# A hybrid gMLP and band-attention step: the norm scaling of va behind the mix, and other places and times for x

## Chip, core and metric

One NeuronCore of a Trainium2 chip runs the whole program. The metric is the device time of one execution in microseconds. The kernel before takes 1076.97 us, the median of three runs (1076.26 to 1078.3).

## What is computed

One layer on 2048 prompt rows and 8 x 16 rows of running streams, 1024 wide, all in float32. The reference, cut to what matters here:

```python
h = einsum('bsd,de->bse', x, w_in)                       # u, va, za, q, k, v, z: 512 columns each
u_a = gelu(u);  v_a = layernorm(gelu(va), ln_v_g, ln_v_b)
mix = einsum('gts,bnsgc->bntgc', tril(w_s), v_a in chunks of 128 rows) + b_s     # 4 groups of 128 channels
a_out = u_a * mix
b_out = band_attention(q, k, v)                          # own 64-row chunk and 8 before, learned bias
out = einsum('bse,ed->bsd', [a_out * silu(za) ; b_out * silu(z)], w_out)
x = layernorm(ALPHA * x + out, ln_g, ln_b)
```

The normalised v_a rows of the 128 stream rows are an output too (gv_out), as are k and v rows. Stream rows use a 16 x 16 corner of each w_s and the first 16 values of b_s.

## The kernel before

A float32 product is made of three in a rounded format: each operand is split by ScalarE into a high part (a Copy with rounding) and by VectorE into a low part (the difference), and TensorE adds high x high, high x low and low x high. Every input block therefore passes ScalarE, then VectorE, before a product can use it.

**Stages.** The rows are cut in 17 tiles of 128 (16 of the prompt, one of the streams).

- *va*: for each tile t, `project_tile` (lines 1647 to 1674) makes x times w_in's va columns, 24 products of 512 columns in two halves h (four blocks of 128 input channels each). Between the halves TensorE does `mix(t - 2)` (lines 1676 to 1685): four small full-precision products, one a group, with w_s transposed. Its PSUM bank alternates between `o_ps` and `out_ps`.
- *First pass*: the columns u, za, k, q, z as ten pairs m of column groups, each a 7-product scheme of Strassen's kind (`product(m, p)`, lines 1687 to 1716, p = 0 to 6) on x transposed, for 1024 rows. A step is one product. The seven combinations of x blocks are made by GpSimd (`sum_x`), those of weights by GpSimd (`sum_w`); both are split as above. The pairs are ("u",0), ("za",0), ("u",2), ("za",2), then k, q, z.
- *v's tiles 0 to 7* with `project_tile`, then the *second pass* (1152 rows, each product in two parts of 288 columns), then *v's tiles 8 to 12*, and tiles 13 to 16 inside the first cycles of the attention, which runs to the end with the output projection.

**Orders written out by hand.** Each engine has its own list of instructions, and semaphores tie them together. What stands where in the lists is what the change touches:

- ScalarE in va (lines 1115 to 1137), for tile t: `copy_mix(t - 2)` (PSUM to the slot `st`, waits until an older mix in that slot is stored), the gelu of tile t, the high half of xt(t + 2, 0), the x pieces planned for t, the high half of xt(t + 2, 1).
- VectorE in va (lines 1404 to 1435): bn_stats (1412), bn_aggr (1414), subtract the mean and multiply with the gain (1416), the low half of xt(t + 2, 0), x pieces, multiply with rstd and add the offset (1425, the norm is then done, semaphore `vn_ready`), the low half of xt(t + 2, 1).
- GpSimd in va (lines 951 to 961): one `sum_x`, the bias of mix(t - 2) (`add_bias_s`, 939), variance plus epsilon (957), the power -1/2 (959).
- SP's queue (lines 703 to 726): the loads of tile t + 2 (595), x for the first pass at t = 0, 2, 5, 8 (601), eight broadcast writes of the relative-bias table to DRAM, `s_skew`, at t = 7 (718), the store of mix(t - 3) to `s_mix` (609).
- In a pass, at step (m, p): unit n = 4m + p - 3 is summed by VectorE once product p is done (`add_sums`, 1360). u units: ScalarE's gelu, then GpSimd's `gate_u` (949) multiplies with `mixb`, the mix loaded back from `s_mix` (619); two buffers alternate, and the load for unit j + 2 is issued after the gate of unit j. za units: tanh on ScalarE (`hand`), two scalings on VectorE (`finish_unit`, 1374 and 1378). Product 1 of the next pair waits for all four sums of the pair, product 6 for the first two. In each step ScalarE and VectorE do `hand` or `finish_unit` first, then the weight splits planned for the step (`step_builds`, lines 1042 and 1334), then the sum.
- x pieces (28 for a pass, split by `xo_high_part` and `xo_low_part`, lines 1054 and 1346): for the first pass 21 in tiles 5 to 15, three in tile 16, four in steps 0 to 3; for the second all 28 in v's tiles 1 to 7 (lines 191 to 197). One group kc of seven pieces needs four sums of GpSimd; a low part waits for all four.
- Token tiles live in three places (`xt_buffer`, 211): 8 KB of `u`, of the `copies`, and, behind tile 8 of v, of the old parameters. For v, tile 0 (8) is loaded in the last pair of the pass, tile 1 (9) after the pass's last sum (lines 751 to 760), since its place is that of the copies.

## Time and profile before

| | |
|---|---|
| median of three runs | 1076.97 us |
| the profiled execution | 1074.96 us |
| its span, first to last instruction | 1073.2 us |
| TensorE matmul busy | 1010.8 us, 94% |
| VectorE busy | 716.9 us, 67% |
| ScalarE busy | 515.6 us, 48% |
| GpSimd busy | 324.6 us, 30% |
| mean granted TensorE clock | 0.979 |

Shares of the whole span mix stages with different limits. TensorE's idle time is 62.4 us in all, and it is read stage by stage: which wait ended last there, and what stood in front of it on the engine waited for.

### The profile page before, as it was taken

How to read it: one execution, taken by the hardware profiler on the slowest of the kernel's cores; microseconds unless marked ns; L12 is line 12 of the kernel's file. 1: busy time of each engine (PE TensorE's matmuls, PEld its weight loads, DVE VectorE, ACT ScalarE, POOL GpSimd, SP SyncE). 2: the span in 40 equal slices, each digit the busy share in tenths (PEclk: the TensorE clock that was granted, in tenths of full speed). 3: DMA queues.
4: the chain of work that ended last, by engine and by line, in shares of the span. 5: the costliest groups of instructions: out<-in, count | busy, mean ns of one | idle time of the engine just before them, and what ended most of it. 6: DMA issues, size and time to landing. Idle time of an engine off the chain costs nothing.

```text
span 1073.2 us, 19266 instructions
## 1 busy us (share of the span) xinstructions
PE 1010.8 (94%) x7456; PEld 865.3 (81%) x7456; DVE 716.9 (67%) x1230; ACT 515.6 (48%) x1018; POOL 324.6 (30%) x269
## 2 busy tenths in 40 slices
PE   7979889999998789999999989999999999999997
PEld 6867677878886569999999977777888888888885
DVE  5959976476565794646555551596777777786765
ACT  5335443334444453333434342575666666666630
POOL 2635753532330834242322200003322222223201
PEclk9998999999999889999999999999999999999999
DMA  6684333346456723323455466575344433433222
GB/s 237 190 232 157 99 108 105 114 121 175 148 145 210 247 94 98 89 92 94 146 175 152 128 200 229 199 261 206 131 149 139 157 133 131 157 121 109 90 80 79
DMA packets 126363, 158.95 MB, mean 148 GB/s; under 512 B 13608, under 2 KB 76224, under 8 KB 126272
## 3 DMA queue, kind: packets, MB, share of 16 engines
q1 hardware_dynamic: 111296, 130.45, 37.8%
q10 hardware_dynamic: 14976, 27.27, 8.0%
q8 instruction: 59, 0.97, 0.4%
q14 instruction: 32, 0.26, 0.1%
HBM read 112.57 MB, written 48.26 MB: 150 GB/s over the span
## 4 chain that ended last, share of the span: by engine, by line
PE 72%; DVE 13%; DMA 6%; issue 3%; ACT 2%; SPq 2%; POOL 1%; ACTq 0%; DVEq 0%
PE s_ps L1713 19%; PE oo_ps L1894 15%; PE pt_ps L1713 9%; PE s_ps L1667 6%; PE oo_ps L1856 6%; PE s_ps L1785 5%; DVE xo_l L1346 4%; PE oo_ps L1713 4%; DMA xt_f<-x_tiles 3%; PE pt_ps L1827 3%; DVE wf L1334 2%; DVE cs L1360 2%; PE s_ps L1894 2%; DVE xt_l L1340 1%; ACT st L1085 1%
## 5 line engine op out<-in xcount | busy, mean ns | idle before, releaser
L1713 PE MATMUL s_ps<-xo_h,wf 128*128 128x288 f32 (+1 forms) x960 | 233.7, 328 | 4.2 <-DVE wf L1334 4.2
L1667 PE MATMUL s_ps<-wp,xt_h 128*128 128x512 f32 x448 | 148.8, 415 | 32.5 <-DVE xt_l L1340 32.0
L1713 PEld LDWEIGHTS s_ps<-xo_h,wf 128*128 128x128 f32 x960 | 164.2, 188 | 17.6 <-DVE xo_l L1346 4.6
L1713 PE MATMUL s_ps<-xo_l,wf 128*128 128x288 f32 (+1 forms) x480 | 157.0, 327 | 0.0
L1667 PEld LDWEIGHTS s_ps<-wp,xt_h 128*128 128x128 f32 x448 | 87.1, 200 | 55.2 <-issue 30.7
L1713 PE MATMUL pt_ps<-xo_h,wf 128*128 128x288 f32 (+1 forms) x480 | 120.8, 329 | 6.8 <-DVE cs L1360 6.6
L1492 DVE CUSTOM_DVE_ANT_1 prob<-s_ps,bias 128x640 f32<-128x640 f32 (+1 forms) x112 | 85.7, 803 | 59.0 <-PE s_ps L1785 59.0
L1228 ACT ACTIVATE prob<-prob,low 128x640 f32<-128x640 f32 (+3 forms) x128 | 97.4, 762 | 45.5 <-DVE low L1492 45.4
L1894 PE MATMUL oo_ps<-wo_h,yh 128*128 128x512 f32 x248 | 100.5, 405 | 0.0
L1334 DVE TENSOR_TENSOR wf<-s,wf 128x512 fp32r<-128x512 f32 x60 | 51.6, 862 | 69.6 <-ACT wf L1042 69.6
L1894 PE MATMUL oo_ps<-wo_h,yl 128*128 128x512 f32 x248 | 97.0, 391 | 0.0
L1894 PE MATMUL oo_ps<-wo_l,yh 128*128 128x512 f32 x248 | 97.0, 391 | 0.0
L1713 PEld LDWEIGHTS pt_ps<-xo_h,wf 128*128 128x128 f32 x480 | 82.3, 188 | 17.2 <-DVE wf L1334 9.0
L1713 PEld LDWEIGHTS s_ps<-xo_l,wf 128*128 128x128 f32 x480 | 90.5, 188 | 6.3
L923 POOL TENSOR_TENSOR s<-a,a 128x512 f32<-128x512 f32 x20 | 26.5, 1323 | 220.3 <-DMA a<-w_pair 220.3
L1667 PE MATMUL s_ps<-wp,xt_l 128*128 128x512 f32 x224 | 91.2, 407 | 0.0
L1334 DVE TENSOR_TENSOR wf<-a,wf 128x512 fp32r<-128x512 f32 x80 | 76.1, 964 | 19.4 <-ACT wf L1042 19.4
L1340 DVE TENSOR_TENSOR xt_l<-xt_f,xt_h 128x512 fp32r<-128x512 f32 x68 | 56.1, 837 | 47.6 <-ACT xt_h L1047 47.6
L1516 DVE TENSOR_SCALAR prob<-prob,rden 128x640 f32<-128x640 f32 (+4 forms) x128 | 79.5, 621 | 4.6
L1713 PE MATMUL pt_ps<-xo_l,wf 128*128 128x288 f32 (+1 forms) x240 | 78.2, 326 | 0.0
L1071 ACT ACTIVATE copy<-s_ps 128x512 f32<-128x512 f32 (+1 forms) x60 | 37.2, 620 | 83.3 <-PE s_ps L1713 83.3
L1002 POOL TENSOR_TENSOR rstd_o<-mv_o,eps 128x1 f32<-128x1 f32 x17 | 3.2, 190 | 235.9 <-DVE mv_o L1567 206.3
(154 smaller groups left out, 2069.1 us busy)
## 6 DMA issues: line engine op xcount, KB each, us to landing
a<-w_pair ACTq DMA_DIRECT2D x80, 256.0 KB, 2.7
xt_f<-x_tiles SPq DMA_DIRECT2D x68, 256.0 KB, 3.3
r<-x SPq DMA_DIRECT2D x17, 512.0 KB, 3.6
s_k<-st SPq DMA_DIRECT2D x32, 256.0 KB, 2.8
s_q<-st SPq DMA_DIRECT2D x32, 256.0 KB, 2.7
q<-s_q SPq DMA_DIRECT2D x16, 512.0 KB, 3.7
k<-s_k SPq DMA_DIRECT2D x16, 512.0 KB, 5.4
y_out<-r SPq DMA_DIRECT2D x15, 512.0 KB, 2.6
```

The source lines that it names most:

```text
L1071: nc.scalar.activation(wide(copies[p // 2], pas), sum_at(p, pas), ACT.Copy).then_inc(copied, 1)
L1228: nc.scalar.activation(prob[s][:, 0:n], prob[s][:, 0:n], ACT.Exp, bias=low[:, s:s + 1], scale=-1.0, accum_out=den[:, s:s + 1]).then_inc(ex ...
L1334: nc.vector.tensor_tensor(wf[:, p, 1], operand[p][:], wf[:, p, 0].bitcast(f32), ALU.subtract).then_inc(w_ready, 1)
L1340: nc.vector.tensor_tensor(xt_l[b][h][:], xt_f[b][h][:], xt_h[b][h][:].bitcast(f32), ALU.subtract).then_inc(xt_ready, 1)
L1346: nc.vector.tensor_tensor(xo_l[a][p][:, kc, :], xo_f[a][p][:, kc, :], xo_h[a][p][:, kc, :].bitcast(f32), ALU.subtract).then_inc(xo_ready, 1)
L1492: nc.vector.tensor_tensor_reduce(out=out, in0=src, in1=b, scale=1.0, scalar=MASKED, op0=ALU.add, op1=ALU.min, accum_out=low[:, s:s + 1]).t ...
L1516: nc.vector.tensor_scalar(prob[s][:, lo:n], prob[s][:, lo:n], rden[:, s:s + 1], None, ALU.mult).then_inc(normed, 1)
L1667: made = nc.tensor.matmul(out, xx[b][h][:, kc % HK, :], wp[:, kc, side, :], start=(h, i, a) == (0, 0, 0), stop=(h, i, a) == (1, HK - 1, 2))
L1713: made = nc.tensor.matmul(out, wf[:, p, side, kc, :], xx[pas][p][:, kc, c * n:(c + 1) * n], start=kc == 0 and a == 0 and p in (0, 1, 3, 5) ...
L1785: last = nc.tensor.matmul(s_ps[h][:, at_c:at_c + count * P], q[t % 2][rows, a * GRP + p, :], key_slots(rows, c * GRP + p, first, count), s ...
L1856: last = nc.tensor.matmul(o_ps[64 * h:64 * h + 64, p * P:(p + 1) * P], v[(t + 1 - nk + b) % KR][:, p * P + 64 * h:p * P + 64 * h + 64], pt ...
L1894: last = nc.tensor.matmul(out_bank(half), y[n % 2][:, c, :], w[h][:, c, :], start=c == 0 and a == 0, stop=c == KC - 1 and a == 2)
```

## The change

- The norm is no longer applied with gain and offset. After the statistics GpSimd also makes shift = -mean * rstd, and ScalarE applies rstd and shift in one instruction (`normalise_va`, ahead of the high half of xt(t + 2, 1)). The gain, a value per channel, commutes with the mix: `scale_mix` multiplies the loaded `mixb` with it on VectorE and adds `mix_b`, which is b_s plus the row sums of w_s times the offset. The row sums are two products of ones with w_s ahead of mix(0); `mix_b` and `mix_bs` (streams) are made on VectorE at its tile 2. GpSimd's bias addition and eight copies for the stream bias go. gv_out gets gain and offset in two VectorE instructions in the first pass's step 1 and is stored from `cs1`.
- x pieces: 16 in va's tiles 3 to 14 and in v's tiles 2, 3, 5, 6; twelve in steps 0 to 3 of each pass. GpSimd makes two `sum_x` a tile; the x loads are at t = 0, 1, 3, 5.
- In a step, ScalarE and VectorE do the splits first, then `hand` or `finish_unit`, then (VectorE) `scale_mix`, then the sum.
- Token halves have seven places. Half 0 of v's tiles 1 and 9 has the place of `mixb`, is loaded in the last pair of the pass and split in its step 4; half 1 is loaded after the last sum but one. The mixes of units 8 and 9 are loaded in v's tiles instead of in the first pass. The first two loads of v for the attention go behind those of tile 12.

The diff, cut:

```diff
+X_FIRST = [(kc, p) for kc in range(HK) for p in range(4)]
+X_REST = [(kc, p) for p in range(4, OPS) for kc in range(HK)]
+for _j, _piece in enumerate(X_FIRST):
+    X_IN_TILE[0].setdefault(3 + 3 * _j // 4, []).append(_piece)
+    X_IN_TILE[1].setdefault((2, 3, 5, 6)[_j // 4], []).append(_piece)
+X_IN_STEP = {step: X_REST[3 * step:3 * step + 3] for step in range(4)}
...
+def xt_place(kind, t, h):
+    if kind == "v" and h == 0 and t in (1, V_MID + 1):
+        return 6
+    if tile_seq(kind, t) % 2:
+        return 2 + h
+    return 4 + h if kind == "v" and t > V_MID else h
...
 (SP)
-                    if j + 2 < len(U_UNITS):
+                    if j + 2 < len(U_UNITS) and j + 2 not in (8, 9):
...
-                    if h == 0 and t in (0, 2, 5, 8):
-                        load_xo(0, (0, 2, 5, 8).index(t))
+                    if h == 0 and t in (0, 1, 3, 5):
+                        load_xo(0, (0, 1, 3, 5).index(t))
...
                             sp.wait_ge(ya_full, 8 * (pas + 1))
+                            sp.wait_ge(u_mixed, 8 * (pas + 1))
                             t = V_MID * pas
                             for h in range(2):
                                 load_xt("v", t, h)
+                            load_xt("v", t + 1, 0)
+                sp.wait_ge(added, 4 * NP * (pas + 1) - 1)
+                load_xt("v", V_MID * pas + 1, 1)
                 store_unit(4 * NP * (pas + 1) - 1)
-                sp.wait_ge(added, 4 * NP * (pas + 1))
-                t = V_MID * pas + 1
-                for h in range(2):
-                    load_xt("v", t, h)
...
-            sp.wait_ge(u_mixed, len(U_UNITS))
-            load_v(0)
-            load_v(1)
             for t in range(V_MID, V_EARLY):
...
+                if t == V_MID + 2:
+                    sp.wait_ge(xt_freed, tile_number("v", V_MID + 1))
+                    load_v(0)
+                    load_v(1)
 (GpSimd)
             for t in range(TILES):
-                if t >= 1:
-                    sum_x(0, t - 1)
-                if t >= 2:
-                    add_bias_s(t - 2)
+                for j in (2 * t - 2, 2 * t - 1):
+                    if 0 <= j < 16:
+                        sum_x(0, j)
                 pool.wait_ge(mv_v_ready, t + 1)
...
+                pool.wait_ge(rstd_v_ready, t + 1)
+                nc.gpsimd.tensor_scalar(shift_v[:], mv_v[:, 0:1], rstd_v[:], -1.0,
+                                        ALU.mult, ALU.mult).then_inc(shift_v_ready, 1)
 (ScalarE)
+            def normalise_va(t):
+                act.wait_ge(shift_v_ready, t + 1)
+                nc.scalar.activation(st[t % 2][:, 0:512], st[t % 2][:, 0:512], ACT.Identity, bias=shift_v[:],
+                                     scale=rstd_v[:]).then_inc(vn_ready, 1)
...
-                    if h == 0 and t < TILES - 1:
+                    if h == 0:
                         for kc, p in X_IN_TILE[0].get(t, ()):
                             xo_high_part(0, kc, p)
+                        normalise_va(t)
...
+                    for what in step_builds(step):
+                        w_high_part(what)
+                    for kc, o in X_IN_STEP.get(step - first, ()):
+                        xo_high_part(pas, kc, o)
                     if p >= 4:
                         hand(4 * m + p - 4)
 (VectorE)
+            def scale_mix(n):
+                if n not in U_COUNT:
+                    return
+                pas, _, g, tb = unit_of(n)
+                j = U_COUNT[n] - 1
+                dve.wait_ge(mix_b_ready, 2 * GRP)
+                dve.wait_ge(mixb_loaded[j % 2], 16 * (j // 2 + 1))
+                held, add = mixb[j % 2][:, 0:512].rearrange("p (n t) -> p n t", t=P), mix_b[:, g, :]
+                made = nc.vector.scalar_tensor_tensor(out=held, in0=held, scalar=v_cols[:, g:g + 1],
+                                                      in1=bass.AP(add.tensor, add.offset, [add.ap[0], [0, 4], [1, P]]),
+                                                      op0=ALU.mult, op1=ALU.add)
+                if pas:
...
+                made.then_inc(mix_scaled, 1)
...
-                nc.vector.scalar_tensor_tensor(out=va, in0=va, scalar=mv_v[:, 0:1], in1=lnvg[:], op0=ALU.subtract,
-                                               op1=ALU.mult).then_inc(vn_centred, 1)
...
-                nc.vector.scalar_tensor_tensor(out=va, in0=va, scalar=rstd_v[:], in1=lnvb[:], op0=ALU.mult,
-                                               op1=ALU.add).then_inc(vn_ready, 1)
                 if t + 2 < TILES:
                     xt_low_part("va", t + 2, 1)
+                if t == 2:
+                    dve.wait_ge(cols_loaded, 32)
+                    dve.wait_ge(row_sums, 2)
+                    for g in range(GRP):
+                        nc.vector.scalar_tensor_tensor(out=mix_b[:, g, :], in0=row_ps[0][:, g * P:(g + 1) * P],
+                                                       scalar=v_cols[:, GRP + g:GRP + g + 1], in1=bs[:, g, :],
+                                                       op0=ALU.mult, op1=ALU.add).then_inc(mix_b_ready, 1)
...
+                    for what in step_builds(step):
+                        w_low_part(what)
+                    for kc, o in X_IN_STEP.get(step - first, ()):
+                        xo_low_part(pas, kc, o)
                     if p >= 4:
                         finish_unit(4 * m + p - 4)
...
+                    if p >= 3:
+                        scale_mix(4 * m + p - 3)
 (TensorE)
                 if t == 0:
                     pe.wait_ge(const_ready, 6)
+                    for row, held in zip(row_ps, (wt, wts)):
+                        nc.tensor.matmul(row[:], st[3][:, 0:P], held[:].rearrange("p g t -> p (g t)"),
+                                         start=True, stop=True).then_inc(row_sums, 1)
                 pe.wait_ge(vn_ready, t + 1)
+                if t == 1:
+                    pe.wait_ge(mix_b_ready, GRP)
```

## Rows read from the trace of the kernel before

**Rows 1.** Busy time by stage: us, PE, PEld, DVE, ACT, POOL, PEclk, DMA, GB/s

```profile
22.60:73.70 51.10, 51.07 (x256) 43.11 (x256) 43.49 (x52) 18.83 (x34) 27.84 (x29) 1.00 0.62 183
...
90.40:133.80 43.40, 39.27 (x192) 31.63 (x190) 42.98 (x48) 20.91 (x38) 28.63 (x28) 1.00 0.40 123
133.80:142.40 8.60, 4.42 (x14) 3.61 (x15) 8.02 (x13) 3.55 (x8) 2.86 (x5) 0.80 0.20 62
142.40:337.70 195.30, 191.73 (x845) 156.44 (x844) 121.94 (x154) 81.87 (x145) 70.72 (x47) 1.00 0.48 141
337.70:404.10 66.40, 50.80 (x194) 39.39 (x192) 52.10 (x52) 32.88 (x58) 32.90 (x19) 0.87 0.52 171
404.10:633.00 228.90, 225.72 (x1689) 224.37 (x1690) 126.36 (x156) 88.51 (x162) 66.45 (x48) 1.00 0.42 125
633.00:672.40 39.40, 32.65 (x138) 25.40 (x136) 11.00 (x20) 13.10 (x24) 0.52 (x1) 0.91 0.69 240
```

**Rows 2.** TensorE's waits over the span: total us, times, longest

```profile
PE s_ps L1667 <- DVE xt_l L1340: 32.0, 9, 7.8
...
PE pt_ps L1713 <- DVE cs L1360: 6.6, 8, 1.0
...
PE s_ps L1713 <- DVE wf L1334: 4.2, 1, 4.2
```

**Rows 3.** Durations of tile st's instructions (ns min/median/max), and one group (mean ns)

```profile
L1412 DVE BATCH_NORM_STATS2 stats_v<-st x17: 673/680/695, 20.3 to 140.2; 128x6 f32<-128x512 f32 x17
...
L1425 DVE SCALAR_TENSOR_TENSOR st<-st,rstd_v,lnvb x17: 736/1757/1781, 23.1 to 142.4; 128x512 f32<-128x512 f32 x17
...
L959 POOL TENSOR_TENSOR rstd_v<-rstd_v,minus_half 128x1 f32<-128x1 f32 x17 | 14.8, 871 | 1.3
```

**Rows 4.** Timeline of va's tiles 2 to 7: start us, us, engine, [idle before]

```profile
29.30 0.60 ACT L1131 ACTIVATE st<-s_ps 128x512 f32<-128x512 f32 x1 [2.14 <-PE s_ps L1667]
...
31.83 1.05 PE L1683 MATMUL oo_ps<-wt,st 128*128 128x128 f32 x8
...
61.04 0.60 ACT L1131 ACTIVATE st<-pt_ps 128x512 f32<-128x512 f32 x1 [1.92 <-PE pt_ps L1667]
```

**Rows 5.** Timeline behind the writes of the bias table

```profile
67.92 3.94 SPq L601 DMA_DIRECT2D xo_f<-x_t  x4
...
77.94 0.60 ACT L1061 ACTIVATE st<-oo_ps 128x512 f32<-128x512 f32 x1 [13.66 <-DMA s_mix<-st]
```

**Rows 6.** Timeline of the first za pair

```profile
175.20 1.77 DVE L1334 TENSOR_TENSOR wf<-a,wf 128x512 fp32r<-128x512 f32 x1
...
177.72 0.47 PE L1713 MATMUL pt_ps<-xo_h,wf 128*128 128x512 f32 x1 [0.88 <-DVE cs L1360]
```

**Rows 7.** First u pair: timeline, the chain's row of product 1, mixb's landing

```profile
155.28 1.75 POOL L949 TENSOR_TENSOR u<-u,mixb 128x512 f32<-128x512 f32 x1
...
158.24 1.75 POOL L949 TENSOR_TENSOR u<-u,mixb 128x512 f32<-128x512 f32 x1
...
161.71 0.68 DVE L1360 TENSOR_TENSOR u<-pt_ps,copy 128x512 f32<-128x512 f32 x1
...
163.24 2.72 PE pt_ps L1713 x12
...
DMA to landing us min/median/max: 2.6/2.7/3.9
```

**Rows 8.** Timeline of v's tiles 1 to 3

```profile
347.98 0.71 PE L1667 MATMUL s_ps<-wp,xt_h 128*128 128x512 f32 x2 [3.66 <-DVE xt_l L1340]
...
351.59 29.24 POOL L905 TENSOR_TENSOR xo_f<-xo_f,xo_f 128x576 f32<-128x576 f32 x16 [34.34 <-DMA xo_f<-x_t]
...
366.69 1.19 PE L1667 MATMUL s_ps<-wp,xt_h 128*128 128x512 f32 x2 [5.92 <-DVE xt_l L1340]
```

**Rows 9.** Timeline of v's tiles 9 and 11

```profile
640.70 1.19 PE L1667 MATMUL s_ps<-wp,xt_h 128*128 128x512 f32 x2 [3.84 <-DVE xt_l L1340]
...
655.87 0.70 PE L1667 MATMUL s_ps<-wp,xt_h 128*128 128x512 f32 x2 [1.50 <-DVE xt_l L1340]
```

More of the change, by code:

```diff
@@ L1150, in _ @@
                         hand(4 * m - 1)
-                    for what in step_builds(step):
-                        w_high_part(what)
-                    for kc, o in X_IN_STEP[pas].get(step - first, ()):
-                        xo_high_part(pas, kc, o)
                     if step == first + 2:
@@ L1398, in _ @@
                 w_low_part(("piece", 0, j))
-            dve.wait_ge(lnv_loaded, 48)
-            for b in range(SB):
-                nc.vector.tensor_copy(bss[:, :, b * SN:(b + 1) * SN], bs[:, :, 0:SN]).then_inc(bss_ready, 1)
+            def scale_mix(n):
[10 more added lines that the diff above has]
+                if pas:
+                    held = mixb[j % 2][:, KEEP:WIDTH[1]]
+                    made = nc.vector.scalar_tensor_tensor(out=held, in0=held, scalar=v_cols[:, g:g + 1],
+                                                          in1=mix_bs[:, g, tb * HALF_S:(tb + 1) * HALF_S],
+                                                          op0=ALU.mult, op1=ALU.add)
+                made.then_inc(mix_scaled, 1)
             for t in range(TILES):
@@ L1444, in _ @@
                         finish_unit(4 * m - 1)
-                    for what in step_builds(step):
-                        w_low_part(what)
-                    for kc, o in X_IN_STEP[pas].get(step - first, ()):
-                        xo_low_part(pas, kc, o)
+                    if p >= 3:
+                        scale_mix(4 * m + p - 3)
                     if m == NP * (pas + 1) - 1 and p in (2, 3):
                         xt_low_part("v", V_MID * pas, p - 2)
+                    if m == NP * (pas + 1) - 1 and p == 4:
+                        xt_low_part("v", V_MID * pas + 1, 0)
                     add_sums(m, p)
@@ L1727, in _ @@
                         pe.wait_ge(xt_high, XT_COUNT["va", t, h])
[L1728 removed]
+                    made = nc.tensor.matmul(tile_ps[t], xt_h[xt_place("va", t, h)][:, j, :], wp[:, kc, 0, :], start=i == 0, stop=False)
                     if i == HK:
@@ L1736, in _ @@
                 for t in range(2):
-                    made = nc.tensor.matmul(tile_ps[t], xt_l[t][h][:, j, :], wp[:, kc, 0, :], start=False, stop=i == KC - 1)
+                    made = nc.tensor.matmul(tile_ps[t], xt_l[xt_place("va", t, h)][:, j, :], wp[:, kc, 0, :], start=False, stop=i == KC - 1)
                     if i == KC - 1:
```

169 lines of the change are left out of this document (85 added, 84 removed).

## The prediction

> **What bounds the kernel now.** I read the table by stage first, then who TensorE waited for, then the timelines of the stages with gaps. The table shows where TensorE is not full [rows 1]. In 22.6 to 73.7 us it is full beside a VectorE busy 43.49 of 51.1 us. In 90.4 to 133.8 VectorE is busy 42.98 of 43.4 us and TensorE 39.27. In 337.7 to 404.1, the first half of v's tiles, TensorE has 50.80 of 66.4 us and a granted clock of 0.87, and in 633.0 to 672.4, the start of the second half, 32.65 of 39.4 at 0.91. The two passes of products are nearly full (191.73 of 195.3, 225.72 of 228.9). So the bound is TensorE, with VectorE taking over in the token stages. The waits say the same: 32.0 us for the low halves of x, 6.6 us in eight waits of about 0.8 us for a sum in the za pairs, 4.2 us once at the first product [rows 2]. Over 0.2%, 2.2 us, can be told from no change here.
>
> A time that recurs below: an undisturbed va tile takes (61.04 - 29.30) / 5 = 6.35 us, its mixing product included [rows 4]. A product takes about 2.8 us in the first pass and 3.2 in the second (195.3 and 228.9 us over 70) [rows 1].
>
> **va's stage, VectorE relieved.** Each tile loses two scalings on VectorE; the second takes 0.74 us alone and 1.76 typically, when GpSimd works beside it [rows 3]. The kept bn_stats takes 0.68, with its aggregate 0.9. The x pieces in this stage fall from 24 to 16, and GpSimd loses its bias addition. VectorE then has at most 0.9 for the statistics, two low halves and two pieces: 0.9 + 4 x 1.76 = 7.9 us at worst, 0.9 + 4 x 0.7 = 3.7 at best, of 6.35. The sixteen GpSimd sums come two a tile up to tile 8 and end there, so from tile 9 the lower figure holds. Six tiles then take 38.1 instead of 43.4 us: gain 5.3. The wait of 4.2 us at the first product goes [rows 2], and with it the low clock: 8.6 us at 0.80 instead of 1.00 are 1.7 us [rows 1]. In tile 8 the low half no longer follows a scaling: 0.8.
>
> What is added lies on ScalarE, the normalising, one instruction of 0.6 us a tile like the others of its size (0.60) [rows 5]. It stands ahead of the high half of xt(t+2, 1) and waits for a chain: gelu 0.6, statistics 0.9, GpSimd's three small instructions 1.3, of which the power is 0.87 [rows 3], normalising 0.6, high 0.6, low 0.7: 4.7, with signals about 5.5 us after a tile's last product. TensorE asks for that half 6.35 + 3.6 = 10 us after it. The cover is 4.5 us; if GpSimd is held by more than that by a late x load, each microsecond beyond is TensorE's.
>
> The Trainium skill, "ScalarE: Activation LUTs", Rules for kernel authors, would leave a multiply and add to VectorE. The stage rows speak for the opposite here, VectorE being the full engine and ScalarE half idle; by the rule the sum would lack the 5.3 us.
>
> **The new wait in tile 3.** mix(1) writes the bank that holds the row sums and so waits until VectorE has made mix_b, which it does at the end of its tile 2, behind both low halves of tile 4. From the gelu of tile 2 at 29.30 [rows 4] the chain of 5.5 us (the gelu included) and four short operations, which I put at 0.25 each (nothing in the trace shows them; below by 0.2, above by 0.7 each), end at 35.8 less signals counted twice, about 35.3. TensorE stood there at 31.83 [rows 4]: 3.5 us. The two row products are 512 columns each like the mix, 0.9 each: 1.8; the earlier start of tile 2 gives 0.8 back. Cost 4.5 us, between 1 and 7. The wait behind s_skew stays: its eight transfers are still queued at tile 7, and ScalarE stood 13.66 us for the store behind them, until 77.94 [rows 5]; x's fourth load is issued at 67.92, behind that store [rows 5], so its move forward frees nothing ahead of it. Net of va: 5.3 + 4.2 + 1.7 + 0.8 - 4.5 = **7.5 us gained**.
>
> **The passes, order of work within a step.** In a za pair VectorE adds, waits for tanh, scales twice, splits a weight and adds again; the split takes 1.77 where GpSimd is beside, and TensorE then waits 0.88 for the sum [rows 6]. The split moves into the wait for tanh, so 0.7 to 1.77 us leave this chain; all 6.6 us of such waits [rows 2] go.
>
> **The passes, the scaling of the loaded mix.** scale_mix now stands on VectorE ahead of the sum, and waits for the load of mixb. That load waits for GpSimd's gate of two units earlier. Today the gates of units 0 and 1 end at 155.28 + 1.75 = 157.0 and 158.24 + 1.75 = 160.0, a load lands 2.7 (2.6 to 3.9) us later, and the sums need none of it [rows 7]. Now unit 2's sum can start at 157.0 + 2.7 + 0.7 = 160.4, unit 3's at 160.0 + 2.7 + 0.7 = 163.4 instead of 161.71, and product 1 of the next pair, which waits until that is done (0.7 more, 164.1), started at 163.24 [rows 7]: 0.9 us in the second u pair of the first pass, none in that of the second, whose steps are longer. In the first pair of a pass twelve x pieces more are split, three a step on ScalarE (3 x 0.55) and VectorE. ScalarE's block loads for the next pair follow them: about 3.4 us later against TensorE, GpSimd's sums and gate behind that. I put 4.0 us in the first pass, where ScalarE also has the last normalising ahead (3.7 us), 0.5 there for the first copy, and 1.5 in the second. Cost 6.9, between 0 and 23 (below). Passes together: **0.3 us lost**. gv_out's two VectorE instructions stand in step 1 and are hidden by product 1 and 2, which need nothing of VectorE's then; without that cover, 1.4. Its store stays on SP at step 2, and behind it only the last mix stores wait.
>
> **v's first half.** Today tile 1 waits 3.66 us for a load issued only when the pass has ended; GpSimd's 16 sums start at 351.59 and take 29.24 us, 1.83 each; VectorE's pieces of the first group stand ahead of tile 3's halves, for which TensorE waits 5.92 us until 366.69 [rows 8]. After: tile 1 is at hand, the sums start some 3 us earlier, VectorE takes xt of tile 3 first and only then four pieces (to 366.8), so that tile 4 is the one that waits, to about 368.7, then tile 5 to 379.6 (4 + 2 operations at 1.83), and the pass starts at about 398 against 404.1. Units 8 and 9's mixes, loaded on SP behind tile 4's halves, are needed only in the second pass, which hides them; ahead of tile 5's halves they would cost about one landing, 2.7. Gain **6.3 us**, between 0 (the slowed pair GpSimd and VectorE still sets the end) and 11.
>
> **v's second half.** The wait of 3.84 at tile 9 goes and so does its low clock [rows 9], but the next tiles then reach the queue of q, k and the bias table earlier: the two v loads of the attention no longer stand ahead of it on SP, and tile 11's load lands about 3 to 4 us earlier, and starts it at about 652.3 instead of 655.87 [rows 9]. Gain **3.6 us**, between 1 and 7.
>
> **Sum.** 7.5 - 0.3 + 6.3 + 3.6 = 17.1. The profiled execution took 1074.96 us (span 1073.2, 1.8 around it), 2.0 below the median of 1076.97; 1074.96 - 17.1 = 1057.9, **1058 us**.
>
> **Rivals.**
> *Port*: scale_mix reads two tiles in SBUF and so may run at 1.76 instead of 0.7 [rows 3] whenever GpSimd sums or gates beside it, as in rows 7. Two in each of four u pairs exposed: 8 x 1.06 = 8.5 us: 1066.5. For it: the gate itself is the neighbour; against: the wait for the load leaves GpSimd idle. The Trainium skill, "SBUF — State Buffer", Who interferes with whom, has exactly this rule, a VectorE instruction with two SBUF inputs blocks against a GpSimd one that reads SBUF; the trace agrees for the old scaling. Chance 0.13.
> *v gives nothing*: the pieces and sums on VectorE and GpSimd still end when they did, the bias table still governs tile 11: 1058 + 9 = 1067. Against it: twelve pieces leave. Chance 0.10.
> *More than I give*: mix_b comes in time and the load chain hides: 4.5 + 6.9 less: 1046.6. For it: half of the costs are estimates. Chance 0.14.
> *Slower*: VectorE's wait for mixb takes the place of all that is saved. Per u pair gate 1.75, load 3.9, scaling 1.76 and sum 0.7 behind block loads that are late too: unit 3 at 17.6 us after product 3 instead of the 10.9 due: 6.7 us, 28 over four pairs instead of my 6.9: 1079. It decides from about 6.5 us a pair. The landing of 2.7 speaks against it. Chance 0.06.
> *No change*: ScalarE, waiting every tile for GpSimd's three small instructions, gives va's gain back and the load chain v's: 1075. Chance 0.04. The forecast itself (1051 to 1065) has 0.53.
>
> **Numbers.** Range 1046 to 1070: it takes in the forecast, both rivals at 1067 and the larger gain, and leaves out slower, no change and the tails. Faster than 1074.8: 0.53 + 0.13 + 0.10 + 0.14 = 0.90; within 0.2% 0.04; slower 0.06.
>
> **What would show it.** Right: no TensorE wait at the first product; a wait of 3 to 4 us at the second mix; VectorE under 0.7 busy in tiles 10 to 16; no eight waits for cs; short waits at product 1 after u pairs; v's pass starts some 60 us after the last product instead of 66. Wrong: TensorE waiting for xt_l in the va tiles behind normalised ones, gaps over 5 us after u pairs, or a v stage as long as now.

## The result, and the profile after

| | before | after |
|---|---|---|
| median | 1077.59 us (1076.26 to 1078.3) | 1069.16 us (1067.01 to 1069.9) |
| ratio | | 0.992, 95% interval 0.9904 to 0.9936 |
| profiled execution's span | 1073.2 us | 1068.1 us |
| granted TensorE clock | 0.979 | 0.983 |

The change makes the kernel 8.4 us faster, 0.8%, where 1058 us was forecast, 17.1 us under the profiled execution of before. The two profiled executions differ by only 5.1 us: the one of before (1074.96) is shorter than all four that its median is made of, and the one of after (1069.9) is the longest of its four. The stage figures below are made against this pair.

The kernel after, busy time by stage (columns as in [rows 1]; the stages begin and end at the same work, not at the same times):

```profile
24.08:72.00 47.92, 42.10 (x194) 34.71 (x193) 25.97 (x42) 22.14 (x40) 25.65 (x31) 0.93 0.46 146
100.15:138.59 38.44, 38.44 (x195) 32.69 (x194) 17.21 (x32) 22.39 (x39) 13.28 (x21) 1.00 0.48 147
138.00:142.40 4.40, 4.40 (x25) 3.77 (x24) 2.53 (x5) 1.71 (x4) 1.57 (x4) 1.00 0.24 60
142.40:339.65 197.25, 190.50 (x835) 155.09 (x834) 140.04 (x171) 87.08 (x156) 66.91 (x45) 1.00 0.47 137
339.65:400.12 60.47, 48.41 (x192) 38.13 (x192) 46.78 (x41) 27.05 (x47) 32.44 (x19) 0.92 0.57 193
400.12:626.89 226.77, 223.68 (x1682) 222.88 (x1681) 144.36 (x180) 93.95 (x171) 68.39 (x45) 1.00 0.43 125
626.89:661.00 34.11, 29.76 (x121) 23.53 (x121) 9.56 (x14) 10.21 (x17) 1.51 (x4) 0.90 0.74 252
```

The second row is the relief of VectorE as it was meant: six tiles take 38.44 us with TensorE full, and VectorE is busy 17.21 us, 0.45 of it. The first row has a fault that [rows 1] did not have: the granted clock of 0.93. TensorE's waits name it (the list of waits of the kernel after):

```profile
PE s_ps L1714 <- DVE xt_l L1355: 26.8, 7, 7.8
...
PE pt_ps L1767 <- DVE u L1377: 7.2, 6, 1.5
PE oo_ps L1735 <- DVE mix_b L1457: 5.8, 1, 5.8
...
PE pt_ps L1767 <- DVE cs L1377: 1.7, 3, 0.9
```

Against [rows 2], the wait of 4.2 us at the first product is gone and the waits for cs fell from 6.6 to 1.7 us. Two others stand in their place, one of 5.8 us for mix_b and six for the sums u, which had none before.

To see where the time comes from, five events are followed through every profile: the start of the first product, the ends of both passes' last products, the start of the second pass, and the first scores. The lengths between them, in us (the last column runs from the first scores to the end of the span):

| kernel | to first product | first pass | v, first half | second pass | v to first scores | rest |
|---|---|---|---|---|---|---|
| before | 137.98 | 199.75 | 66.32 | 227.19 | 35.73 | 406.2 |
| after | 138.03 | 201.62 | 60.47 | 226.77 | 34.11 | 407.1 |
| order alone | 141.83 | 196.39 | 66.93 | 222.84 | 35.57 | 403.5 |
| no scaling | 137.80 | 196.45 | 62.10 | 224.31 | 34.42 | 405.3 |
| old order | 136.71 | 209.87 | 59.46 | 240.62 | 34.21 | 406.3 |
| all pieces in v | 135.75 | 201.57 | 66.63 | 224.89 | 35.65 | 407.4 |
| tile 1 late | 136.54 | 200.90 | 64.67 | 226.90 | 33.79 | 405.3 |
| own bank | 128.27 | 201.77 | 60.70 | 226.70 | 34.64 | 406.1 |
| made sooner | 128.59 | 200.60 | 60.67 | 226.66 | 34.55 | 404.4 |
| late table | 120.71 | 200.85 | 59.65 | 226.72 | 34.61 | 408.2 |
| scale after sum | 122.07 | 198.76 | 61.04 | 222.83 | 34.99 | 404.7 |
| tile 11 early | 119.19 | 201.08 | 60.11 | 226.75 | 30.43 | 406.5 |
| all three | 121.74 | 199.08 | 57.47 | 222.93 | 30.23 | 405.9 |

The table also shows its own scatter. Where nothing was edited, the first column repeats within 3.9 us (137.98 and 141.83 in the kernel before and the order alone, which are the same up to there; 119.19 to 122.07 in the four kernels with the late table, 135.75 to 138.03 in the kernel after and four others), the first pass within 1.2, the second within 0.3, v's halves within 2.6 and 0.9, the rest within some 5. Differences under these are read only where a row of the timeline shows what they are made of.

Before against after, the gain lies in v's first half (5.9 us) and second half (1.6). va's stage gained nothing up to its end: the first product starts at 138.03 instead of 137.98. What is left of it is the clock behind that point. Before, the first 4.42 us of products have a granted clock of 0.66, which is 1.5 us lost, and after it is 1.00; so the first pass, 1.87 us longer by the table, really lost 3.4.

### The profile page after: what moved, and what is told of

Its sections match the earlier page's. It is cut to its first block, busy times and chain, and to the rows that moved or that the text cites. A ratio compares the mean times of both kernels' runs of the same rounds, so it can differ in the third digit from the quotient of the medians.

```text
span 1068.1 us, 19316 instructions
## 1 busy us (share of the span) xinstructions
PE 1010.1 (95%) x7460; PEld 866.4 (81%) x7460; DVE 695.8 (65%) x1222; ACT 526.7 (49%) x1035; POOL 304.6 (29%) x269
## 4 chain that ended last, share of the span: by engine, by line
PE 73%; DMA 8%; DVE 7%; issue 3%; POOL 3%; SPq 3%; ACT 2%; ACTq 0%; DVEq 0%; POOLq 0%
PE s_ps L1767 17%; PE oo_ps L1948 15%; PE pt_ps L1767 9%; PE s_ps L1714 8%; PE oo_ps L1910 6%; PE s_ps L1839 5%; PE oo_ps L1767 3%; PE pt_ps L1881 3%; DMA xt_f<-x_tiles 2%; PE pt_ps L1714 2%; PE s_ps L1948 2%; POOL xo_f L925 1%; DMA wp_raw<-w_tok 1%; PE s_ps L1868 1%; PE oo_ps L1735 1%
## 5 line engine op out<-in xcount | busy, mean ns | idle before, releaser
L1355 DVE TENSOR_TENSOR xt_l<-xt_f,xt_h 128x512 fp32r<-128x512 f32 x68 | 63.7, 949 | 82.7 <-ACT xt_h L1057 82.4
L1349 DVE TENSOR_TENSOR wf<-a,wf 128x512 fp32r<-128x512 f32 x80 | 62.2, 797 | 24.3 <-ACT wf L1052 24.3
L1910 PE MATMUL oo_ps<-pt,v 128*64 128x128 f32 x1120 | 68.8, 276 | 2.1 <-ACT pt L1235 2.1
```

Source lines behind the costliest of these rows:

```text
L1349: nc.vector.tensor_tensor(wf[:, p, 1], operand[p][:], wf[:, p, 0].bitcast(f32), ALU.subtract).then_inc(w_ready, 1)
L1355: nc.vector.tensor_tensor(xt_l[b][:], xt_f[b][:], xt_h[b][:].bitcast(f32), ALU.subtract).then_inc(xt_ready, 1)
L1910: last = nc.tensor.matmul(o_ps[64 * h:64 * h + 64, p * P:(p + 1) * P], v[(t + 1 - nk + b) % KR][:, p * P + 64 * h:p * P + 64 * h + 64], pt ...
```

## The experiments

### The wait in tile 3

The kernel after, timeline from tile 2's gelu (start us, us, engine):

```profile
30.24 0.60 ACT L1144 ACTIVATE st<-s_ps 128x512 f32<-128x512 f32 x1
...
31.94 0.68 DVE L1442 BATCH_NORM_STATS2 stats_v<-st 128x6 f32<-128x512 f32 x1
...
34.19 0.26 POOL L972 TENSOR_SCALAR shift_v<-mv_v,rstd_v 128x1 f32<-128x1 f32 x1
...
34.48 0.81 ACT L1075 ACTIVATE st<-st,shift_v,rstd_v 128x512 f32<-128x512 f32 x1 [3.13 <-POOL shift_v L972]
35.20 0.61 ACT L1057 ACTIVATE xt_h<-xt_f 128x512 fp32r<-128x512 f32 x1
35.85 1.71 DVE L1355 TENSOR_TENSOR xt_l<-xt_f,xt_h 128x512 fp32r<-128x512 f32 x1 [2.44 <-ACT xt_h L1057]
37.48 1.11 DVE L1457 SCALAR_TENSOR_TENSOR mix_b<-oo_ps,v_cols,bs 128x128 f32<-128x128 f32 x4
...
38.74 2.04 PE L1735 MATMUL oo_ps<-wt,st 128*128 128x128 f32 x8 [5.82 <-DVE mix_b L1457]
...
45.46 0.60 ACT L1144 ACTIVATE st<-pt_ps 128x512 f32<-128x512 f32 x1 [4.04 <-PE pt_ps L1714]
```

The chain is the one the forecast walked: gelu, statistics, GpSimd's small instructions, normalising, high half, low half, mix_b. Tile 3 ends 15.22 us after tile 2 (45.46 - 30.24) instead of 6.35, that is 8.87 lost. The wait is 5.82 of it, and the other 3.05 is the clock: after the wait the mix takes 2.04 us instead of 1.05, and the second half of the tile runs at the lower level. The same kernel, busy time in the wait, behind it, and in tile 4:

```profile
32.90:38.74 5.84, 0.02 (x1) 0.03 (x1) 3.40 (x7) 1.33 (x2) 3.84 (x5) 0.93 0.00 0
38.74:45.46 6.72, 6.72 (x21) 5.71 (x22) 0.89 (x4) 0.60 (x1) 0.00 (x0) 0.55 0.44 142
45.46:51.83 6.37, 6.37 (x33) 5.40 (x32) 4.13 (x6) 3.97 (x7) 4.24 (x5) 1.00 0.56 180
```

The granted clock is 0.55 in the 6.72 us behind the wait (1.2 GHz for nearly all of it) and full again in the next tile.

**A bank of its own.** The row sums go to a bank that nothing uses in this stage.

```diff
-        row_ps = [out_ps, pt_both[:, 1].rearrange("p g t -> p (g t)")]
+        row_ps = [s_ps[0][:, 0:512], pt_both[:, 1].rearrange("p g t -> p (g t)")]
...
-                if t == 1:
-                    pe.wait_ge(mix_b_ready, GRP)
...
-                    if p == 1:
-                        pe.wait_ge(mix_b_ready, 2 * GRP)
+                    if p == 0 and not pas:
+                        pe.wait_ge(mix_b_ready, 2 * GRP)
```

> The kernel after, but the row sums of w_s go to a bank of s_ps that nothing uses in va's stage, so that mix(1) no longer waits for mix_b; product 0 of the first pass waits for it instead, long after it is made. Theory (the wait in tile 3 ate va's gain): the row oo_ps <- mix_b (5.8 us) goes, tile 3 takes about 6.4 us instead of 15.2, the gelu of tile 7 comes at about 62 instead of 70.87, and all that follows with it: 8 to 9 us less than the kernel after's 1069, so 1060 to 1061. Rival (another wait stands behind it: the low half of tile 5 behind the making of mix_b on VectorE, or the transfers of the bias table, which take a fixed time): the wait turns up for xt_l in tiles 5 to 9, and under 4 us are gained, 1065 to 1069.

Measured: 1059.09 us (1054.73 to 1059.95), ratio to before 0.9821 (0.9797 to 0.9844). In its timeline mix(1) waits for nothing, while mix_b is made later than it:

```profile
30.27 0.60 ACT L1144 ACTIVATE st<-s_ps 128x512 f32<-128x512 f32 x1
...
32.79 1.05 PE L1733 MATMUL oo_ps<-wt,st 128*128 128x128 f32 x8
...
36.61 0.60 ACT L1144 ACTIVATE st<-pt_ps 128x512 f32<-128x512 f32 x1 [0.26 <-PE pt_ps L1714]
37.59 1.11 DVE L1457 SCALAR_TENSOR_TENSOR mix_b<-s_ps,v_cols,bs 128x128 f32<-128x128 f32 x4
```

Tile 3 takes 6.34 us, 8.9 less, and no other stage moves. The first product starts 9.8 us earlier (128.27) and the median is 10.1 lower; what these have beyond 8.9 is within the scatter. So one borrowed bank cost some 9 us, and it was what va's gain had gone to.

**mix_b made sooner.** The kernel after, the eight operations for mix_b and mix_bs at the head of VectorE's tile 2, bank and wait as they are.

```diff
+                if t == 2:
+                    dve.wait_ge(cols_loaded, 32)
+                    dve.wait_ge(row_sums, 2)
...
                 dve.wait_ge(tile_evac, t + 1)
                 nc.vector.bn_stats(stats_v[:], va).then_inc(stats_ready, 1)
...
                     xt_low_part("va", t + 2, 1)
-                if t == 2:
-                    dve.wait_ge(cols_loaded, 32)
-                    dve.wait_ge(row_sums, 2)
...
```

> The kernel after, mix_b made at the head of VectorE's tile 2 instead of at its end, in the same bank and with the same wait. The row products end at about 26.5 us and VectorE is free at about 32, so four of its eight operations of 0.28 us end at about 33, when TensorE comes to mix(1). Theory (the wait is for VectorE's place in its own list): a wait of under 1 us at mix(1), no slow clock, 8 to 9 us gained, 1060 to 1061, like the experiment with a bank of its own. Rival (the statistics of tile 2, now 2.2 us later, make tile 4's second half late): the wait moves to xt_l in tile 4, 4 to 6 us gained.

Measured: 1062.02 us (1057.22 to 1063.43), ratio 0.9861 (0.9834 to 0.9889). The same timeline:

```profile
31.72 1.11 DVE L1445 SCALAR_TENSOR_TENSOR mix_b<-oo_ps,v_cols,bs 128x128 f32<-128x128 f32 x4
...
32.97 1.13 PE L1735 MATMUL oo_ps<-wt,st 128*128 128x128 f32 x8 [0.28 <-DVE mix_b L1445]
```

A wait of 0.28 us, and the first product at 128.59, though the median is only 7.1 us under the kernel after's. What was expensive was neither the row sums nor their making, but the last place of its tile in VectorE's list, behind a chain that goes through GpSimd and ScalarE.

### The stall behind the bias table's writes

In [rows 5] ScalarE stood 13.66 us for a store behind the eight writes of s_skew. After, it stands 12.44 and TensorE 7.80. I had put this stall down as one that stays. The next run moves the writes, on the kernel with a bank of its own.

```diff
-                if t == 7:
-                    sp.wait_ge(rel_stored, 32)
-                    for h in range(HEADS):
-                        sp.dma_start(s_skew[h, :, 0:REL], s_rel[h, :].partition_broadcast(P)).then_inc(rel_stored, 16)
...
+                        if pas == 0 and p == 3 and m in (4, 5, 6, 7):
+                            sp.wait_ge(rel_stored, 32)
+                            for h in (2 * m - 8, 2 * m - 7):
+                                sp.dma_start(s_skew[h, :, 0:REL], s_rel[h, :].partition_broadcast(P)).then_inc(rel_stored, 16)
```

> The first experiment's kernel, and the eight broadcast writes of the bias table moved from tile 7 of va to the k and q pairs of the first pass, two at a time. If the wait of 7.8 us for xt_l in tile 9 or so is the queue of these writes, it goes: 7 to 9 us less than the first experiment, about 1052 to 1054, and the passes are not longer, since their transfers have slack. If VectorE and ScalarE were the bound there anyway, under 3 us are gained; if the writes hurt the stores and block loads of the pass, waits for a block or a store appear there and the gain is given back.

Measured: 1051.08 us (1049.34 to 1053.3), ratio 0.9752 (0.9729 to 0.9775): 8.0 us less than with the own bank. The gelus of tiles 7 to 10 come every 6.35 us; the first and the last of them:

```profile
63.79 0.60 ACT L1144 ACTIVATE st<-pt_ps 128x512 f32<-128x512 f32 x1 [0.92 <-PE pt_ps L1714]
...
82.83 0.60 ACT L1144 ACTIVATE st<-s_ps 128x512 f32<-128x512 f32 x1 [1.00 <-PE s_ps L1714]
```

The first pass is not longer (200.85 against 201.77). So the stall came from these writes, and none of it was VectorE's. The kernel after, busy time in the stall (the last two numbers are the share of the DMA engines and GB/s):

```profile
78.00:90.00 12.00, 5.53 (x29) 4.39 (x27) 0.30 (x1) 1.42 (x3) 0.00 (x0) 0.82 1.04 288
```

The DMA engines are full there, where the kernel with the moved writes has a share of 0.54 from 62 to 88 us. Whether the store was late for its place behind the writes in SP's queue or for the full engines is not shown; the run takes away both.

### The passes: order of work, and the scaled mix

**The order alone**, on the kernel before; ScalarE is shown, and VectorE is changed alike with w_low_part, xo_low_part and finish_unit.

```diff
+                    for what in step_builds(step):
+                        w_high_part(what)
+                    for kc, o in X_IN_STEP[pas].get(step - first, ()):
+                        xo_high_part(pas, kc, o)
                     if p >= 4:
                         hand(4 * m + p - 4)
                     if p == 0 and step > first:
                         hand(4 * m - 1)
-                    for what in step_builds(step):
-                        w_high_part(what)
-                    for kc, o in X_IN_STEP[pas].get(step - first, ()):
-                        xo_high_part(pas, kc, o)
```

> The kernel before with one part of the change alone: in a step of a pass ScalarE and VectorE do the splits first and then hand or finish_unit. Theory (the forecast's term): the eight waits for cs, 6.6 us, go, and the time falls by 5 to 6.6 us, to 1071 to 1072.5. Rival (the splits ahead of the tanh and the gelu make the u sums and products late, so that waits for u take their place): 1 to 3 us gained, or nothing, 1075 to 1077, and a row PE <- u in the list of waits.

Measured: 1067.72 us (1066.86 to 1068.85), ratio 0.991 (0.9895 to 0.9924). The waits for cs fall from 6.6 to 1.2 us, those for u do not appear:

```profile
PE s_ps L1713 <- DVE wf L1334: 4.2, 1, 4.2
...
PE pt_ps L1713 <- DVE cs L1360: 1.2, 2, 0.7
```

The passes take 3.36 and 4.35 us less, 7.7 together, more than the 5 to 6.6 that I expected. (The median is 10.5 us under that of the kernel before in the same series; what this has beyond 7.7 lies in stages that were not edited, and is not read.) This reordering of a few lines does by itself as much as the whole change, 0.991 against 0.992.

**No scaling**, on the kernel after.

```diff
-                    if p >= 3:
-                        scale_mix(4 * m + p - 3)
...
-                pool.wait_ge(mix_scaled, j + 1)
+                pool.wait_ge(mixb_loaded[j % 2], 16 * (j // 2 + 1))
```

> The kernel after without the scaling of the loaded mix (the gain, the offset's row sums and b_s are left out of the gating); GpSimd's gate waits for the load alone, as in the kernel before. Theory (the forecast's rival Port, now half seen: the scalings at 1.78 us and their wait for the load make the u sums late): the 7.2 us of waits for u shrink to under 2 us and the time falls by 4 to 6 us from the kernel after's 1069, to 1063 to 1065. Rival (the twelve x pieces in steps 0 to 3 are what is late): waits for u stay above 5 us and under 2 us are gained.

Measured: 1060.95 us (1059.46 to 1062.17), ratio 0.9846 (0.983 to 0.9861). Its list of waits has no row for u, and the passes take 5.17 and 2.46 us less than after, 7.6 together, where I expected 4 to 6 in all. The kernel after, timeline of the first u pair:

```profile
145.39 0.47 PE L1767 MATMUL s_ps<-xo_h,wf 128*128 128x512 f32 x1 [0.85 <-ACT copy L1086]
...
152.17 2.07 POOL L943 TENSOR_TENSOR s<-a,a 128x512 f32<-128x512 f32 x1 [9.07 <-DMA a<-w_pair]
153.00 1.78 DVE L1426 SCALAR_TENSOR_TENSOR mixb<-mixb,v_cols,mix_b 128x512 f32<-128x512 f32 x1
...
154.70 0.68 DVE L1377 TENSOR_TENSOR u<-s_ps,copy 128x512 f32<-128x512 f32 x1
...
156.41 1.78 DVE L1426 SCALAR_TENSOR_TENSOR mixb<-mixb,v_cols,mix_b 128x512 f32<-128x512 f32 x1
...
158.11 0.68 DVE L1377 TENSOR_TENSOR u<-pt_ps,copy 128x512 f32<-128x512 f32 x1
...
158.94 0.47 PE L1767 MATMUL pt_ps<-xo_h,wf 128*128 128x512 f32 x1 [1.48 <-DVE u L1377]
...
160.34 1.24 DVE L1426 SCALAR_TENSOR_TENSOR mixb<-mixb,v_cols,mix_b 128x512 f32<-128x512 f32 x1 [0.46 <-DMA mixb<-s_mix]
...
163.68 1.30 DVE L1426 SCALAR_TENSOR_TENSOR mixb<-mixb,v_cols,mix_b 128x512 f32<-128x512 f32 x1 [0.40 <-DMA mixb<-s_mix]
164.91 0.68 DVE L1377 TENSOR_TENSOR u<-pt_ps,copy 128x512 f32<-128x512 f32 x1
...
165.73 0.47 PE L1767 MATMUL pt_ps<-xo_h,wf 128*128 128x512 f32 x1 [1.10 <-DVE u L1377]
```

Each sum stands behind a scaling, the first two of 1.78 us. The second sum ends at 158.79 and product 6 starts behind it, a wait of 1.48 that I had not listed. Of the load itself the scalings wait 0.46 and 0.40 us. The x pieces and the last normalising are not quite free either. The kernel without scaling, which still has them, takes 196.45 us for its first pass, and the order alone, which has neither, 196.39; but the order alone begins it with 4.42 us at a granted clock of 0.68 (1.4 us lost) and the other at 1.00. So they cost up to 1.5 us, and 0.85 of it can be seen: the wait for ScalarE's copy at 145.39, which the kernel without scaling has too and neither the order alone nor the kernel before has.

**Scale after the sum**, on the kernel with the late table.

```diff
-                    if p >= 3:
-                        scale_mix(4 * m + p - 3)
...
                     add_sums(m, p)
+                    if p >= 3:
+                        scale_mix(4 * m + p - 3)
```

> The fourth experiment's kernel with one call moved: in a step VectorE adds the unit's sum first and scales the loaded mix behind it, instead of the other way. Theory (what the scaling costs is that the u sums stand behind it and behind its wait for the load; 5.2 and 2.5 us in the two passes by the kernel that left it out): the waits for u, 7.5 us, go nearly all, the first pass takes about 196.5 us instead of 200.85 and the second about 224.5 instead of 226.7, in all 1044 to 1046. Rival (the scaling itself, at 1.78 us beside GpSimd, fills VectorE and delays gate, tanh and product 1 wherever it stands): under 2 us gained, 1049 to 1051.

Measured: 1044.56 us (1042.29 to 1046.1), ratio 0.9694 (0.9676 to 0.9712), 6.5 us less than its base. All of the scaling is still done, and 2.1 and 3.9 us of the passes are back. The eight scalings of the first pass take 9.1 us in sum, against 10.4 ahead of the sums. Its waits:

```profile
PE pt_ps L1765 <- DVE u L1377: 1.3, 2, 1.1
...
DVE mixb L1426 <- DMA mixb<-s_mix: 1.0, 1, 1.0
```

So it was the place ahead of the sum that cost, more than the work.

**The old order**, the same part undone inside the whole change (the diff of the order alone, backwards, on the kernel after).

> The kernel after with one part undone: in a step hand and finish_unit stand ahead of the splits again. Theory (the new order is worth 7.7 us, as it was alone): the waits for cs come back, six to eight of 0.8 us, the passes take 7 to 8 us more (201.6 and 226.8 now), 1076 to 1077, which is no gain over the kernel before. Rival (inside the whole change the scaled mix governs the pairs, the order brings little): 1070 to 1072.

Measured: 1090.21 us (1088.95 to 1091.7), ratio 1.0136 (1.0114 to 1.0158). Both expectations are far off: the passes take 8.3 and 13.9 us more than after, 22.1 in all, and the change becomes a loss. In its list of waits the two kinds stand side by side:

```profile
PE pt_ps L1767 <- DVE u L1377: 16.0, 8, 3.1
PE pt_ps L1767 <- DVE cs L1377: 7.0, 9, 0.9
```

The order is worth 7.7 us to the kernel before and 22 to the kernel after. Of the 22, 16.0 - 7.2 = 8.8 are longer waits for u and 7.0 - 1.7 = 5.3 waits for cs, by their rows. Most of the rest is clock, which falls behind the longest of these waits (3.02, 2.96 and 3.14 us). The same kernel, busy time behind the three:

```profile
159.13:163.23 4.10, 4.10 (x11) 3.27 (x12) 3.03 (x3) 1.04 (x2) 2.95 (x2) 0.58 0.45 128
428.23:432.88 4.65, 4.65 (x24) 4.65 (x25) 3.52 (x4) 1.10 (x2) 3.10 (x2) 0.63 0.43 120
488.42:494.32 5.90, 5.90 (x25) 5.90 (x26) 2.84 (x3) 2.77 (x5) 1.41 (x1) 0.50 0.29 89
```

TensorE is full in them at 0.58, 0.63 and 0.50, which is 1.7, 1.7 and 3.0 us lost, 6.4 in all; the kernel after has 1.00 in both passes. That leaves 1.6 us.

### v's first half

**All pieces in v**: the kernel after, the second pass's 28 x pieces in tiles 1 to 7 again.

```diff
-    X_IN_TILE[1].setdefault((2, 3, 5, 6)[_j // 4], []).append(_piece)
+for _j in range(28):
+    X_IN_TILE[1].setdefault(min(1 + _j // 4, V_MID - 1), []).append((_j // 7, _j % 7))
+X_IN_STEP = [{step: X_REST[3 * step:3 * step + 3] for step in range(4)}, {}]
```

> The kernel after with all 28 x pieces of the second pass in v's tiles 1 to 7 again, as in the kernel before, and none in its steps. Theory (the pieces set v's first half): 64 to 67 us from the last product of the first pass to the second pass instead of 60.5, the second pass 0 to 1.5 us shorter, 1072 to 1075. Rival (tile 1's place alone gives the 6 us): 60 to 62 us, 1067 to 1070.

Measured: 1072.31 us (1071.17 to 1073.64), ratio 0.9954 (0.9938 to 0.9969). v's first half takes 66.63 us, as long as before, and the second pass 1.9 less.

**Tile 1 late**: the kernel after, v's tiles 1 and 9 loaded behind the pass's last sum, as before, and their half 0 split there too.

```diff
-                            load_xt("v", t + 1, 0)
...
+                sp.wait_ge(added, 4 * NP * (pas + 1))
+                for h in range(2):
+                    load_xt("v", V_MID * pas + 1, h)
```

> The kernel after with one part undone: the first halves of v's tiles 1 and 9 are loaded and split after the pass as in the kernel before, in the place that the change gave them. Theory (v's first half gains from the twelve x pieces that left it, since the chain that ends last is x's load, GpSimd's sums and VectorE's pieces, and tile 1 stands beside it): the wait of 3 us at tile 1 is back, but the second pass starts within 1 us of the kernel after, 60 to 61.5 us after the last product; in v's second half 1 to 2 us are lost; 1070 to 1072. Rival (tile 1 at hand is what gives): 63 to 65 us there, 1073 to 1075.

Measured: 1068.91 us (1065.0 to 1071.63), ratio 0.9915 (0.9884 to 0.9947). The time can't be told from the kernel after's, but the stage can: 64.67 us against 60.47. My theory for this run is wrong and its rival right. GpSimd's first sum starts 14.4 us after the last product there and 12.2 after it here:

```profile
351.89 29.01 POOL L925 TENSOR_TENSOR xo_f<-xo_f,xo_f 128x576 f32<-128x576 f32 x16 [33.25 <-DMA xo_f<-x_t]
...
355.47 1.19 PE L1714 MATMUL s_ps<-wp,xt_h 128*128 128x512 f32 x2 [3.16 <-DVE xt_l L1355]
...
370.40 0.70 PE L1714 MATMUL s_ps<-wp,xt_h 128*128 128x512 f32 x2 [2.24 <-DVE xt_l L1355]
...
381.60 1.19 PE L1714 MATMUL s_ps<-wp,xt_h 128*128 128x512 f32 x2 [5.50 <-DVE xt_l L1355]
```

(The rows are the kernel after's.) Undoing tile 1's place alone costs 4.2 us and undoing the pieces alone 6.2, where both together had given 5.9, so they need each other. My reading, which no run isolates, is that tile 1 at hand lets x's loads and the sums start sooner, and the fewer pieces let VectorE use that.

### v's second half

**Tile 11 early**, on the kernel with the late table.

```diff
                 load_xt("v", V_MID + 2, h)
+            sp.wait_ge(added, NUNITS)
+            load_xt("v", V_MID + 3, 0)
...
             load_qk(1)
+            store_v(V_MID)
+            load_xt("v", V_MID + 3, 1)
             sp.wait_ge(rel_stored, 16 * (2 + HEADS))
```

> The fourth experiment's kernel with v's tile 11 loaded earlier: its first half behind tile 10's, ahead of q, k and the bias table, its second half ahead of the bias table. Theory (v's second half gained 1.6 to 1.7 us instead of 3.6, because tile 11's load stands behind that table's transfer): TensorE's wait at tile 11 (4 us and the slow clock after it) goes, first scores 3 to 5 us earlier against the end of the second pass (34.6 us now), the time 1046 to 1048. Rival (what moved behind is late next: q and k, the bias table, tile 12): first scores at most 1 us earlier, 1050 to 1051.

Measured: 1046.78 us (1045.89 to 1049.21), ratio 0.972 (0.9702 to 0.9737). The first scores come 30.43 us after the second pass instead of 34.61, 4.2 less. The kernel after, TensorE at tile 11, where [rows 9] had 1.50:

```profile
647.85 1.19 PE L1714 MATMUL s_ps<-wp,xt_h 128*128 128x512 f32 x2 [4.35 <-DVE xt_l L1355]
```

This wait of 4.35 us is gone in the experiment; 0.86 us in tile 11's second half and 1.75 in tile 12 stand in its place, and the clock stays at 1.00. In the kernel after, tile 11's load was issued at 638.56, behind the bias table's load and a store. Tile 11 starts 20.96 us after the pass's last product, where it was 24.63 before, so it does come 3.7 us sooner; but TensorE is at hand earlier still, and the long wait and the low clock behind it moved from tile 9 to tile 11. Busy time from tile 11's start to the first scores, after and before:

```profile
647.85:661.00 13.15, 13.15 (x49) 10.41 (x50) 3.23 (x5) 3.26 (x6) 0.00 (x0) 0.83 0.45 146
655.87:666.97 11.10, 11.10 (x48) 8.90 (x49) 3.23 (x5) 3.30 (x6) 0.00 (x0) 1.00 0.41 133
```

The same work takes 2.05 us longer at a granted clock of 0.83 instead of 1.00, and of the 3.7 us only 1.6 are left.

### All of it together

"Scale after sum" and "tile 11 early", and the first x load of the second pass ahead of the store of the first pass's last unit:

```diff
                 load_xt("v", V_MID * pas + 1, 1)
+                if pas == 0:
+                    sp.wait_ge(proj_done, DONE["f", NP - 1, OPS - 1])
+                    load_xo(1, 0)
                 store_unit(4 * NP * (pas + 1) - 1)
```

> The fifth experiment's kernel, with tile 11's loads of the sixth, and the first x load of the second pass ahead of the store of the first pass's last unit on SP. The first adds 4 us to v's second half if the parts are independent (30.4 instead of 35.0 us to the first scores), the second 2 to 3.5 us to v's first half, because GpSimd's sums, the head of the chain that ends it, start that much sooner (61.0 to about 58 us): 1037 to 1039. Rival for the second: the loads of tiles 2 and 3 stand behind it and are late in its place, nothing gained: 1040 to 1041.

Measured: 1038.25 us (1035.18 to 1039.0), ratio 0.9643 (0.9623 to 0.9663), the shortest time of all runs: 3.6% under the kernel before, and 31 us under the one after. v's first half takes 57.47 us and GpSimd's sums start 9.65 us after the last product, at 330.47.

## Why the prediction was right or wrong

The direction and the range held; the size was more than twice what was measured. By the forecast's terms:

- **va, the relief of VectorE, 5.3 us: right.** Six tiles in 38.44 us against 43.4, so 5.0. The wait at the first product went (4.2), and its slow clock: the first 4.4 us of products run at 1.00 instead of 0.66, 1.5 us where I had 1.7.
- **va, "the new wait in tile 3", 4.5 us: the step that failed.** It cost 9.8 us: a wait of 5.82, 3.05 of clock, and 0.9 for the row products (from tile 0's gelu to tile 2's it is 10.60 us instead of 9.66), against 3.5, nothing and 1.0 in the sum. The mechanism, the place and the chain were as told, the size was not. The wait was 5.8 instead of 3.5: VectorE started on tile 2's statistics at 31.94, 1.7 us behind the gelu's start, because a low half of 1.76 and two instructions for the bias table stood ahead; the normalising took 0.81 instead of 0.6; the low half 1.71 where I had 0.7. (The short operations, which I had put at 0.25 each without a row, took 1.11 us for four, 0.28 each.) The other half of the error is that the sum had no term for the clock. I credited 1.7 us of clock for a wait of 4.2 that goes, and charged none for a wait that comes: 3.05 us. The Trainium skill, "ScalarE: Activation LUTs", What ACT_TABLE_LOAD costs, says of an ACTIVATE that each `[128,1]` pointer operand adds about 93 ns; the normalising has two, and the rows agree (0.81 against 0.60 for the gelu).
- **The stall behind s_skew stays: right**, 13.66 before and 12.44 after, but naming it as fixed left 8 us lying that one moved loop takes. **Tile 8, 0.8: not there.** From tile 7's gelu to tile 10's it is 29.3 us after and 29.4 before.
- **Passes, "all 6.6 us of such waits go": right, and low**; 7.7 alone, and of the waits 1.7 us are left in the kernel after.
- **Passes, "the scaling of the loaded mix": mis-sized.** I had 0.9 us for it in the second u pair and 0.5 for the first copy, with 4.0 on x pieces. It took 7.6 us in both passes by the run without it, and the pieces with the last normalising up to 1.5 in the first pass and 1.9 in the second (I had 1.5). The total of costs was 10.6 against 6.9 (5.23 and 3.93 between the order alone and after, and the 1.4 us of slow clock that only the order alone has), and its parts were further off than the total. I looked only for the load's wait and product 1; the scaling itself, at 1.78 us, delays the second sum, for which product 6 waits.
- **The rival Port** had this mechanism and its price, 8.5 us. Its 1066.5 is nearer to the result than the forecast, but mostly by luck: of the 12 us by which the sum missed the difference of the spans, the passes are 2.7 and va 6.0. The Trainium skill, "SBUF — State Buffer", Who interferes with whom, says that a VectorE instruction with two SBUF inputs and a GpSimd one that reads SBUF block each other. The 1.78 beside a GpSimd sum at 153.00 agrees, and so does the 0.75 of the one at 193.75, where GpSimd is idle. But behind the sum the scalings still take 0.85 to 1.20 in the first pair, and 6 of the 7.6 us are saved. So moving them is enough; how much of the wait ahead of the sum is due to their longer duration, no run shows.
- **The rival Slower** had the size of what the old order shows, 21 us more than the forecast's cost in the passes against 22.1, but not its mechanism: in that run VectorE never waits for mixb. The change escaped this loss only because of the new order, and the forecast took the two as separate terms to be added.
- **v's first half, 6.3: right**, 5.9. **Second half, 3.6: high**, 1.6. Tile 9's wait of 3.84 went, and tile 11 started 3.7 us earlier, as forecast. But its own wait grew from 1.50 to 4.35, and the clock behind it cost 2.05 us: the same missing term as in tile 3.

Summed: 1.5 from va where 7.5 were forecast (the start of the first product is unchanged, only the clock behind it is gained), 3.0 lost in the passes instead of 0.3, 5.9 and 1.6 gained in v, and 0.9 lost in the rest, which is within its scatter: 5.1, the difference of the two spans. Of the 12 us that are missing, the wait in tile 3 has 5.3, the passes 2.7 and the clock behind tile 11's wait 2.05.

## What to carry to other kernels

When a change borrows a resource for a short task (a bank, a slot), the price is where the task's last reader stands in its engine's list, not how long the task takes: 2.2 us of VectorE's work cost some 9 us here, and next to nothing in a free bank, or earlier in the same list. A wait of several microseconds on TensorE is charged twice, once as itself and once for the clock behind it, both when it goes and when it comes; behind waits of 4.2, 4.35 and 5.8 us it was 1.5, 2.1 and 3.05 us here. And two parts of a change on one engine's list are not terms to be added: run each alone and each undone, since the order was worth 7.7 us without the scaled mix and 22 with it.

## What was not expected of the hardware

- A wait of 5.82 us on TensorE was followed by a granted clock of 0.55 over 6.72 us, and 3.05 us were lost to it in one tile, half as much as the wait.
- Eight DRAM writes queued on SP held ScalarE 11 to 14 us for a store behind them in all nine profiles that have them there (13.7 before, 12.4 after, 11.1 to 14.3 in the other seven), and cost TensorE 8 us by the run that moved them; two at a time, in a stage with slack, they cost nothing that can be measured.
- GpSimd's power of a 128x1 operand took 0.55 us in tiles 0 to 2, 15 and 16, and 0.88 to 0.92 in tiles 3 to 14, where VectorE splits x pieces beside it; I took 0.87 throughout.
